# Prompt attention: three PSUM banks for turned tiles, one for outputs

## The reference, cut to what matters

```
# A, 16 heads in 4 groups: compressed (c), selected (s) and sliding (w) keys
s = einsum(q, k) * scale + bias[distance];  p = masked_softmax(s)
o_A = g[0] * (p_c @ v_c) + g[1] * (p_s @ v_s) + g[2] * (p_w @ v_w)
# B, 8 differential heads, two maps each
a = masked_softmax(s1) - lam * masked_softmax(s2)
o_B = rmsnorm(a @ v)
o = sigmoid(ga) * o_A + sigmoid(gb) * o_B
```

## Time and profile before

| what | us |
|---|---|
| median of 3 runs | 1606.74 (1606.26 to 1613.9) |
| the profiled execution's own time | 1612.34 |
| its span | 1610.5 |
| matmuls busy in the span | 1513.5 |
| VectorE busy | 849.6 |
| ScalarE busy | 604.1 |

### The profile page before, as it was taken

How to read it: one execution, slowest core, us unless ns; L and a number is a source line. 1 busy time by engine, 2 the same in 40 slices (tenths; PEclk the granted TensorE clock), 3 DMA queues, 4 the chain that set the end, 5 groups by cost and what they waited for, 6 DMA issues and landing times. The chain is left out here.

```text
span 1610.5 us, 31774 instructions
## 1 busy us (share of the span) xinstructions
PE 1513.5 (94%) x12648; PEld 1262.9 (78%) x12648; DVE 849.6 (53%) x1814; ACT 604.1 (38%) x1165; POOL 186.6 (12%) x269
## 2 busy tenths in 40 slices
PE   8999999999899978898887988999899999999998
PEld 5888888877799966665555757676679999999998
DVE  4866533214798748777785534545454432244322
ACT  5322211314454437666764323333433321133210
POOL 1000000000544100083421000000000000000000
PEclk9999999999899999999998989989899999999999
DMA  7635468544333275334422999998624334343321
GB/s 209 200 121 175 152 248 297 187 104 98 85 110 112 60 199 160 72 131 125 144 80 81 371 363 361 364 335 306 238 67 130 106 112 123 104 130 117 92 78 56
DMA packets 186010, 265.79 MB, mean 165 GB/s; under 512 B 36381, under 2 KB 117725, under 8 KB 185766
## 3 DMA queue, kind: packets, MB, share of 16 engines
q1 hardware_dynamic: 174930, 227.27, 43.3%
q0 software_dynamic: 6016, 25.34, 5.3%
q10 hardware_dynamic: 4948, 11.62, 2.0%
HBM read 241.11 MB, written 42.60 MB: 176 GB/s over the span
## 5 line engine op out<-in xcount | busy, mean ns | idle before, releaser
L751 PE MATMUL pj_ps<-all_hi,pj_xh 128*128 128x512 f32 x480 | 192.0, 400 | 0.2 <-DVE all_lo L623 0.2
L753 PE MATMUL pj_ps<-all_hi,pj_xl 128*128 128x512 f32 x480 | 189.9, 396 | 0.0
L752 PE MATMUL pj_ps<-all_lo,pj_xh 128*128 128x512 f32 x480 | 189.8, 395 | 0.0
L3178 PE MATMUL fi_ps<-fi_th,fi_wh 128*128 128x272 f32 x512 | 147.6, 288 | 1.7 <-DVE fi_tl L2935 1.7
L3179 PE MATMUL fi_ps<-fi_fl,fi_wh 128*128 128x272 f32 x512 | 148.5, 290 | 0.0
L3180 PE MATMUL fi_ps<-fi_th,fi_wl 128*128 128x272 f32 x512 | 148.3, 290 | 0.0
L3178 PE MATMUL fi_ps<-fi_fh,fi_wh 128*128 128x272 f32 x512 | 147.8, 289 | 0.0
L3180 PE MATMUL fi_ps<-fi_fh,fi_wl 128*128 128x272 f32 x512 | 147.6, 288 | 0.0
L3179 PE MATMUL fi_ps<-fi_tl,fi_wh 128*128 128x272 f32 x512 | 147.2, 287 | 0.0
L2493 ACT ACTIVATE de_slot<-de_ps_t 128x512 f32<-128x512 f32 (+5 forms) x124 | 62.8, 513 | 176.9 <-PE de_ps_t L2327 92.6
L2603 DVE COPY de_slot<-de_ps_t 128x512 f32<-128x512 f32 (+4 forms) x112 | 68.7, 622 | 111.4 <-PE de_ps_t L2327 66.5
(11 more groups left out here) (406 smaller groups left out, 3325.1 us busy)
## 6 DMA issues: line engine op xcount, KB each, us to landing
de_dv<-in_cache_diff SPq DMA_DIRECT2D x64, 512.0 KB, 9.9
all_big<-in_w_in SPq DMA_DIRECT2D x14, 2048.0 KB, 9.7
de_dk<-in_cache_diff SPq DMA_DIRECT2D x48, 512.0 KB, 9.9
all_big<-in_cache_nsa SPq DMA_DIRECT2D x64, 256.0 KB, 6.4
all_big<-in_w_up SPq DMA_DIRECT2D x16, 1024.0 KB, 5.6
all_big<-in_w_down SPq DMA_DIRECT2D x16, 1024.0 KB, 5.6
all_dk<-in_cache_diff SPq DMA_DIRECT2D x16, 512.0 KB, 8.0
all_win<-in_cache_win SPq DMA_DIRECT2D x32, 256.0 KB, 7.5
```

The costliest lines, as they stand in the source:

```text
L751: pe.matmul(ps[:, t, :], xh[:, k, xk], wh[:, u, k, :], start=k == 0, stop=False)
L752: pe.matmul(ps[:, t, :], xh[:, k, xk], wl[:, u, k, :], start=False, stop=False)
L753: return pe.matmul(ps[:, t, :], xl[:, k, xk], wh[:, u, k, :], start=False, stop=k == KT - 1)
L3178: pe.matmul(o, hi[:, k, :], a_hi[:, k, tok], start=k == 0, stop=False)
```

## The change

`ps_t` gets a third bank: entry r takes bank r mod 3 and waits for the copy of entry r-3. `ps_o` is a single bank. Heads write to its first and second quarter in turn, tiles to its halves in turn. Since writing and reading one bank at the same time isn't allowed, `values` of a pair of heads waits until both heads of the pair before are read, `combine_head` waits until both of its pair are made, and `wide_values` of tile m waits on a new semaphore, `out_read`, which counts the reads of VectorE, until tile m-1 is read (before: tile m-2 combined). The last tile and the third from the end are written to the score banks 0 and 2, once all scores are read; the one between them then waits for the tile two before.

VectorE's step order changes: before, scaling, copy of the fourth tile, then the three operations of the combining; after, copy, first operation of the combining (the read), scaling, the two additions. The read no longer waits for its own end at once; the additions do.

```diff
-        ps_t = s.ps("ps_t", [P, 2, CW])
-        ps_o = s.ps("ps_o", [P, 2, CW])
+        ps_t = s.ps("ps_t", [P, 3, CW])
+        ps_o = s.ps("ps_o", [P, CW])
...
-                self.out = [ps_o[:, n % 2, 0:DV]]
+                self.out = [ps_o[:, DV * (n % 2):DV * (n % 2 + 1)]]
...
-                self.wide = ps_o[:, self.tile % 2, 0:2 * P].rearrange("p (h c) -> p h c", h=2)
+                last = 2 * QT * GROUPS - 1 - self.m
+                bank = ps_s[:, last, :] if last in (0, 2) else ps_o
+                self.wide_flat = bank[:, 2 * P * (self.tile % 2):2 * P * (self.tile % 2 + 1)]
+                self.wide = self.wide_flat.rearrange("p (h c) -> p h c", h=2)
...
-                if r >= 2:
-                    pe.wait_ge(copied[copier[r - 2]], copies[r - 2])
-                return ps_t[:, r % 2, :]
+                if r >= 3:
+                    pe.wait_ge(copied[copier[r - 3]], copies[r - 3])
+                return ps_t[:, r % 3, :]
...
             def wide_values(x):
-                pe.wait_ge(combined, x.tile - 1)
+                last = 2 * QT * GROUPS - 1 - x.m
+                if last in (0, 2):
+                    pe.wait_ge(scored, 2 * N)
+                elif last == 1:
+                    pe.wait_ge(out_read, x.m - 1)
+                elif x.m:
+                    pe.wait_ge(out_read, x.m)
+                else:
+                    pe.wait_ge(combined, NH)
                 stand()
...
             def values(x):
-                if x.opens_tile and x.tile >= 2:
-                    pe.wait_ge(combined, x.tile - 1)
+                if x.n >= 2:
+                    pe.wait_ge(combined, x.n - x.n % 2)
                     stand()
...
             def combine_head(x):
-                dve.wait_ge(valued, x.n + 1)
+                dve.wait_ge(valued, x.n - x.n % 2 + 2)
...
-                step(nc.vector.tensor_tensor(part[:].rearrange("p h b e -> p (h b) e"),
-                                             ps_o[:, x.tile % 2, 0:2 * P].rearrange("p (b e) -> p b e", e=DK),
-                                             coef[:, x.m % 4, :].unsqueeze(2).to_broadcast([P, 4, DK]), ALU.mult))
+                nc.vector.tensor_tensor(part[:].rearrange("p h b e -> p (h b) e"),
+                                        x.wide_flat.rearrange("p (b e) -> p b e", e=DK),
+                                        coef[:, x.m % 4, :].unsqueeze(2).to_broadcast([P, 4, DK]), ALU.mult).then_inc(out_read, 1)
+
+            def sum_branches(x):
+                dve.wait_ge(out_read, x.m + 1)
...
                 if NH <= j - LAG < N:
                     if j - LAG == NH:
                         combine_head(UNITS[NH - 2])
-                    scale_branches(UNITS[j - LAG + 1])
                     copy(UNITS[j - LAG + 1])
                     if j - LAG == NH:
                         combine_head(UNITS[NH - 1])
                 if NH <= j - LAG - 2 < N:
                     combine_branches(UNITS[j - LAG - 1])
+                if NH <= j - LAG < N:
+                    scale_branches(UNITS[j - LAG + 1])
+                if NH <= j - LAG - 2 < N:
+                    sum_branches(UNITS[j - LAG - 1])
```

More of the change, by code:

```diff
@@ L1388, in prompt_attention @@
         oa_out = shared.oa_out
-        pool_step = s.sem("pool_step")
+        pool_step, out_read = s.sem("pool_step"), s.sem("out_read")
         o_sq, o_root, ob_scale = s.sem("o_sq"), s.sem("o_root"), s.sem("ob_scale")
@@ L1767, in fill_copy @@
                 out = place_of(x)
-                nc.scalar.activation(out, ps_t[:, r % 2, 0:out.shape[1]], ACT.Copy).then_inc(copied["act"], 1)
+                nc.scalar.activation(out, ps_t[:, r % 3, 0:out.shape[1]], ACT.Copy).then_inc(copied["act"], 1)
             def wide_copy(x):
@@ L1784, in copy @@
                         act.wait_ge(turned, r + 1)
-                        nc.scalar.activation(x.p_t[a][:, 0:w], ps_t[:, r % 2, 0:w], ACT.Copy).then_inc(copied["act"], 1)
+                        nc.scalar.activation(x.p_t[a][:, 0:w], ps_t[:, r % 3, 0:w], ACT.Copy).then_inc(copied["act"], 1)
             fill_copy(("q", 0, 0))
@@ L1840, in cmp_scores @@
                 nc.vector.tensor_tensor(cmp_p.rearrange("p (t h c) -> p t h c", t=QT, h=HPG)[:, :, half::2, :],
-                                        ps_t[:, r % 2, 0:2 * CHP * QT].rearrange("p (t h c) -> p t h c", t=QT, h=2), bias,
+                                        ps_t[:, r % 3, 0:2 * CHP * QT].rearrange("p (t h c) -> p t h c", t=QT, h=2), bias,
                                         ALU.add).then_inc(copied["dve"], 1)
@@ L1867, in cmp_outputs @@
                 pair = slice(2 * half, 2 * half + 2)
-                nc.vector.tensor_tensor(cmp_o[:, pair, :, :], ps_t[:, r % 2, :].rearrange("p (t h e) -> p t h e", t=2, h=HPG),
+                nc.vector.tensor_tensor(cmp_o[:, pair, :, :], ps_t[:, r % 3, :].rearrange("p (t h e) -> p t h e", t=2, h=HPG),
                                         cmp_coef[:, 2 * HPG * half:2 * HPG * (half + 1)].rearrange("p (t h) -> p t h", t=2)
@@ L1893, in fill_copy @@
                 out = place_of(x)
-                nc.vector.tensor_copy(out, ps_t[:, r % 2, 0:out.shape[1]]).then_inc(copied["dve"], 1)
+                nc.vector.tensor_copy(out, ps_t[:, r % 3, 0:out.shape[1]]).then_inc(copied["dve"], 1)
             def copy(x):
@@ L1900, in copy @@
                 rows, w = x.values[0].shape[0], P * len(x.values)
-                nc.vector.tensor_copy(x.p_t[1][0:rows, 0:w], ps_t[0:rows, r % 2, 0:w]).then_inc(copied["dve"], 1)
+                nc.vector.tensor_copy(x.p_t[1][0:rows, 0:w], ps_t[0:rows, r % 3, 0:w]).then_inc(copied["dve"], 1)
             def mix_maps(n):
```

## The result

The changed kernel takes 1598.32 us (median of 6 runs, 1595.88 to 1599.08); the kernel before took 1610.97 us on the same chip (6 runs, 1606.26 to 1615.64). The ratio is 0.9931, 95% interval 0.9909 to 0.9953: 11 us less, from 8 to 15 (the two medians differ by 12.7). The forecast was 11.7 us less, 1595.0, with a range of 1587 to 1604. The profiled execution took 1598.93 us with a span of 1597.1.

A forecast was written before the change was run, and what follows sets the result against it. TensorE was taken to bound the prompt attention, so its idle spells count: 7.5 us from the groups' part and 4.2 from the heads' part, 11.7 off the median of 1606.74, gave 1595.0 us, range 1587 to 1604.

The forecast's parts named there:

- The third bank: Groups' part, pair m: one turn's start distance gained, 0.17, 0.28, 0.39, 0.48 us at m mod 4 of 0 to 3.
- The output bank's price: Product of pair m waits for VectorE's read of m-1, then five queue steps of 0.15 us: 0.75 us behind read's end.
- t=2 with nothing between: Pairs 6, 14, 22, 26 (t = m mod 4, no fill): 0.13 us lost each, 0.4 at 6; 0.8 together.
- Compressed probabilities: Pairs 7, 15, 23, with compressed probabilities slipped in: VectorE late, so the earlier read pays; 1.0 us gained.
- Compressed outputs: Pairs 0, 8, 16, 24: the fill goes at once, turns wait for VectorE's output copies; 2.3 us gained.
- ScalarE's lateness: Groups' part: 1.0 us taken off for four more pairs where ScalarE isn't waiting ahead of its output copy.
- The heads' part: Part with eight differential heads: TensorE's 5.5 us of waits go, but VectorE limits the regular rounds; 4.2 us gained.
- The regular rounds: Heads' part, three rounds of four heads, VectorE all but full: 0.39 us gained each, 1.2 together.
- The rounds with group fills: Heads' part, pairs loaded with group fills, bound by TensorE: 3.0 us gained with overlaps.
- the wait only moves: Rival: ScalarE's third copy and VectorE hold the pairs; 5.3 us gained, heads give nothing, 1601.4 us; chance 22%.
- Slower: Rival: VectorE comes late to the read, so the output bank is the bound; 1615 us; chance 6%.
- The free output bank: Rival: the output bank costs nothing and all waits but 3 us go; 20 us gained, 1587 us; chance 12%.

The follow-up runs named there:

- the first two experiments: Changed kernel with turned tiles waiting for the entry two before again, everywhere (1615.8 us, ratio 1.0064), then in the groups' part only (1611.04 us, 1.0040).
- all three edits: Changed kernel with third group's loads issued before the squares' wait, fewer waits ahead of products (read last), third tile's copy ahead of exps: 1588.56 us, again 1586.93 us.

## Why the prediction was right

**The third bank** gives each pair one turn's start distance: confirmed to 0.02 us where nothing else is late (pairs 3, 11, 19 by 0.48 to 0.50; the first two experiments give them back). The waits for a bank of turned tiles fell from 17.5 to 9.6 us (7.4 + 2.2), not to 4: 4.4 us are VectorE's chain to the compressed outputs, which the prediction put at 3, and 2.2 the loads. The waits ahead of products rose from 4.4 to 8.6 us (forecast: 4 to 10).

**The output bank's price**, five steps of 0.15 us behind the read, is what was found: 0.75 us ahead of six products, 0.90 ahead of two, 0.75 at the tail when it is put there, and gone when the read's wait comes last and steps are left out. Its total the prediction never stated; it stood in the sum as forgone gain. The profiles give 5.4 us for it together with VectorE's new order. At t=2 with nothing between I forecast +0.13 for each of four; 14, 22, 26 show +0.08, +0.23, +0.23. The forecast for pair 6 was +0.4, and it took 0.47 less; but 1.9 us of it were at the lower clock before, so at most a part of that is the change. The prediction also has the product of tile 27 wait for tile copies alone; the rows above show it held by the read of tile 26. The size came out near (-0.32 for -0.24) all the same.

**Compressed probabilities** (7, 15, 23): 1.0 us forecast, nothing came. Their transposition now waits for ScalarE, which it didn't before; TensorE after, ahead of the product of tile 23:

```profile
816.77 0.63 PE L1650 MATMUL pa_ps_t<-all_ident,all_win 128*128 128x128 f32 x4 [0.19 <-ACT all_win L1814]
817.52 0.40 PE L1724 MATMUL pa_ps_o<-pa_p_t,pa_vs 128*64 128x256 f32 x1
```

0.2 us at each of the three, and the five steps stand behind the fill: 0.75 us from its release to the product again. I had asked only whether VectorE was in time, and forgot the fill's own input.

**Compressed outputs**: 2.3 us forecast. Where the loads had landed, pairs 0+1 and 16+17 gained 1.8 and 2.1 against 0.9 each; 24+25 nothing against 0.3. Neither gain is clean: 16+17 had 3.4 us at the lower clock before, and pair 0 took 9.08 or 9.09 us instead of 7.77 in three other kernels whose VectorE has the same instructions there. For tile 8 the prediction had no row: the load of the third group was no releaser of anything before. This is the step that failed, and at 1.7 us (pair 8, shown by the early loads at the full clock) it was larger than the error of the whole sum. That the sum of -6.4 lies so near to -7.5 is luck in part: misses of both signs cancel, such as -0.7 at t=2 with nothing and the 1.0 us taken off for ScalarE's lateness, against +1.0 at the compressed probabilities and the 1.7 us of the load.

**The heads' part**: 4.2 us forecast, 7.2 in the profiles. The regular rounds are right: from the value product of head 10 to that of head 14 8.37 us before and 7.92 after, 0.45 where I had 0.39. The one at 621.93 in the earlier trace rows answers to this after, a round later, with VectorE's reads ahead of it:

```profile
629.71 0.83 PE L1743 MATMUL pa_ps_o<-all_big,pa_p_t 128*128 128x128 f32 x6
...
628.77 0.61 DVE L1934 TENSOR_SCALAR pa_ob<-pa_ps_o,pa_mix 128x128 f32<-128x128 f32 x2
```

0.33 us behind the second read's end. The rounds with group fills, from head 14 to head 26, gave 4.0 against 3.0, but before had 3.4 us of them at the lower clock (666.0 to 669.4). The rest I put down to the part's beginning and to the clock: before had 16.3 us of the part at the lower level, after 11.5. Eleven profiled kernels had three banks in the heads' part with the same instructions in it: 81.1 to 83.9 us, mean 82.4. Two had two banks: 88.3 and 87.0. By that the part is worth 5.3 us, between the forecast and the single pair of profiles. Added to the groups' 6.4 it gives 11.7 us, the very sum of the forecast, with one part 1.1 us under its own and the other 1.1 over.

**The rivals.** That the wait only moves (1601.4) is refuted: it left nothing to the heads' part, and its 5.3 us lie outside the interval of 8 to 15. Slower (1615) is refuted for the changed kernel. With one output bank and two turned ones the time is 1615.8 us, but not by that rival's way, a VectorE that comes late to its reads: there the products stand 0.75 to 0.91 us behind the read at t=2 as in the changed kernel, and the third bank's gain is missing. The free output bank (1587) is refuted by the time and by the waits behind the reads; the kernel with fewer steps takes 1591 us, and the one with all three edits is where that rival had put it, by other ways than it named.

On the halves of one bank: the prediction weighed the Trainium skill's rule (PSUM — Partial Sum Buffer, "PSUM bank collisions raise a hardware error") that PSUM is guarded by bank. No run here let the two engines into one bank together, so the rule itself is not tested. The kernel has the wait in its code; the forecast with it was 11.7 us and without it 14.1, and both lie in the interval of 8 to 15, so it is the rows behind the reads and not the time that show the wait.

**Open**: why what follows the stage took 738.4 us before and 730.2 to 736.5 in twelve others. It is the same code, there is one profile of before, and the four medians of before, one beside each set of kernels, were 1605.89 to 1610.97. Open too are why the two kernels without the third bank in the groups' part took some 5 us more than their parts add up to, what makes 0.90 us of 0.75 at some products, and what makes pair 0 1.3 us longer in three profiles: there four of VectorE's small operations took 1.91 us instead of 1.06.

## What to carry to other kernels

When banks are moved from one use to another, price both: list for each use who frees it and when, and count what stands in the consumer's queue behind that wait, as here five short waiting steps put every held product 0.75 us behind its release. Put the wait that comes last in time last in the queue, and leave out waits that a later one covers. And when a wait is removed, ask for the next input of the instruction that it held, loads included: one that was never late before has no row in the profile, so look for where its issue stands in its queue and what that waits for.

## What the runs showed of the hardware

Five semaphore waits, each with an instruction that only counts, took 0.75 us of TensorE's queue from the event that ended the first of them, at six products (0.90 at two more). That is 0.15 us for each on average, an estimate that takes in the way of the first signal. The profile calls it "issue" or puts it down to no one. The lower clock level (1.2 GHz) cost 0.13 to 0.28 us per microsecond in this stage. Pairs 4 and 5 took 7.69 and 5.20 us after, with 6.9 us of them at the lower level, and 6.80 and 4.18 us at the full one (2.4 GHz) in the kernel with early loads, which has the same instructions there: 1.91 us for 6.9. Pair 21 took 4.62 us after, with 3.4 us at the lower level, and 4.17 at the full one: 0.45 us for 3.4. The stretches fall elsewhere in each execution, and in the heads' part alone moved the length of the same code by up to 2.8 us; that is why parts of a stage are compared over several profiles, or pair by pair.
